# Query norms as softmax scale columns, and queries and keys of a head in turn, in a hybrid attention and mixture-of-experts block

## What is computed

```python
q = rms_norm(q.reshape(B, S, DSA_HEADS, DSA_HEAD_DIM), q_norm_g)
k = rms_norm(k.reshape(B, S, DSA_HEADS, DSA_HEAD_DIM), k_norm_g)
...
logits = jnp.einsum('bqhd,bqkhd->bqhk', qb, k_sel) * (DSA_HEAD_DIM ** -0.5)
logits = jnp.where(valid[:, :, None, :], logits, -jnp.inf)
p = jax.nn.softmax(logits, axis=-1)
```

## Time and profile before

| what | value |
|---|---|
| median of 3 runs | 1149.65 us (1147.72 to 1150.21) |
| profiled execution | 1148.97 us, its span 1147.2 us |
| PE busy | 1094.4 us, 95% |
| DVE busy | 562.6 us, 49% |
| ACT busy | 333.0 us, 29% |
| POOL busy | 263.6 us, 23% |
| moved by DMA | 263.77 MB |

### The profile page before, as it was taken

The page is one execution under the profiler, slowest core; times in us unless marked ns, Lnnn a source line. Parts: engine busy times, 40 slices in busy tenths (PEclk is TensorE's granted clock), DMA queues, the critical chain, the costliest instruction groups (busy, mean ns, idle before and its releaser), DMA issues.

```text
span 1147.2 us, 14250 instructions
## 1 busy us (share of the span) xinstructions
PE 1094.4 (95%) x5694; PEld 709.1 (62%) x5694; DVE 562.6 (49%) x1040; ACT 333.0 (29%) x595; POOL 263.6 (23%) x168
## 2 busy tenths in 40 slices
PE   7999999999999999999999958999999999999997
PEld 5779899767689887878877733333333333333332
DVE  4332693498880243348994452333344433333334
ACT  6344723333332455551224301111111111111111
POOL 7423244333223444453334010000000000000000
PEclk9999999999999999999999969999999999999999
DMA  7222233322214322235318489999999999999995
GB/s 190 74 56 75 73 83 102 92 56 74 74 38 111 78 71 55 57 107 186 110 37 351 182 342 410 421 420 420 419 421 421 420 420 420 420 422 420 421 421 230
DMA packets 129617, 263.77 MB, mean 230 GB/s; under 512 B 12736, under 2 KB 98752, under 8 KB 104976
## 3 DMA queue, kind: packets, MB, share of 16 engines
q1 hardware_dynamic: 125376, 255.23, 59.7%
q0 software_dynamic: 2496, 4.50, 1.1%
q10 hardware_dynamic: 1680, 3.15, 0.7%
HBM read 262.85 MB, written 4.20 MB: 233 GB/s over the span
## 4 chain that ended last, share of the span: by engine, by line
PE 69%; SPq 17%; DVE 6%; DMA 3%; issue 1%; ACT 1%; POOL 1%; DVEq 0%; POOLq 0%; ACTq 0%
PE bank L502 15%; PE bank L523 14%; PE bank L870 10%; SPq L435 9%; PE bank L750 8%; PE bank L884 5%; SPq L436 5%; PE bank L811 3%; SPq L444 3%; DMA arena<-w_exp_up_in 3%; DVE work L1354 2%; PE bank L890 2%; PE bank L706 1%; PE bank L689 1%; PE bank L891 1%
## 5 line engine op out<-in xcount | busy, mean ns | idle before, releaser
L1768 POOL TENSOR_TENSOR piece_r<-arena,piece_r 128x1024 fp32r<-128x1024 f32 x84 | 202.1, 2413 | 329.0 <-ACT piece_r L973 328.9
L870 PE MATMUL bank<-arena,work 128*64 128x512 f32 x1024 | 230.8, 600 | 11.5 <-DMA arena<-w_exp_up_in 10.4
L502 PE MATMUL bank<-piece_r 128*128 128x512 f32 x936 | 232.2, 399 | 0.0
L502 PEld LDWEIGHTS bank<-piece_r 128*128 128x128 f32 x936 | 171.1, 188 | 40.2 <-issue 6.9
L870 PEld LDWEIGHTS bank<-arena,work 128*64 128x64 f32 x1024 | 70.5, 137 | 156.1 <-issue 133.8
L523 PEld LDWEIGHTS bank<-piece_r 128*128 128x128 f32 x1344 | 162.0, 192 | 6.1 <-issue 6.1
L523 PE MATMUL bank<-piece_r 128*128 128x256 f32 x1344 | 164.9, 284 | 0.0
L1640 DVE TENSOR_TENSOR arena<-bank,arena 128x512 f32<-128x512 f32 x128 | 81.8, 683 | 99.1 <-PE bank L891 99.1
L973 ACT ACTIVATE piece_r<-arena 128x1024 fp32r<-128x1024 f32 x84 | 88.4, 1057 | 124.2 <-DMA arena<-w_in_in 68.7
L884 PE MATMUL bank<-arena,bias 128*64 128x512 f32 x512 | 116.9, 598 | 1.6 <-ACT bias L1209 1.4
L1830 POOL DMA_INDIRECT arena<-x_rows,idx_pair x16 | 16.0, 998 | 393.7 <-PE bank L859 345.3
(11 more groups left out here) (244 smaller groups left out, 1085.0 us busy)
## 6 DMA issues: line engine op xcount, KB each, us to landing
arena<-w_exp_gate_in SPq DMA_DIRECT2D x64, 1024.0 KB, 26.1
arena<-w_exp_up_in SPq DMA_DIRECT2D x64, 1024.0 KB, 26.8
arena<-w_exp_down_in SPq DMA_DIRECT2D x32, 2048.0 KB, 29.0
arena<-w_in_in SPq DMA_DIRECT2D x68, 512.0 KB, 3.9
arena<-w_branch_gla_in SPq DMA_DIRECT2D x8, 512.0 KB, 3.9
arena<-w_branch_dsa_in SPq DMA_DIRECT2D x8, 512.0 KB, 5.1
arena<-w_out_in SPq DMA_DIRECT2D x2, 2048.0 KB, 12.6
arena<-x_in SPq DMA_DIRECT2D x4, 512.0 KB, 5.0
```

Source lines behind the costliest of these rows:

```text
L502: last = mm(bank[n % 2][:, :], w[:, k, :], h[:, k, :], start=(i == 0 and k == 0), stop=(i == 2 and k == K - 1))
L870: last = mm(bank[0][hf * WIDE:(hf + 1) * WIDE, :], hTe[q][:, k, :], wgu[sl][2][:, :, k, hf * HALF:(hf + 1) * HALF], start=(k == 0), stop=( ...
L1768: Q.tensor_tensor(quarter(w_lo, q), quarter(w_raw, q), quarter(w_hi, q).bitcast(F32), ALU.subtract).then_inc(s["wlo_ready"], 1)
```

## The change

Queries and keys of a head now come in turn: tile j belongs to head j // 2, and is a query tile for even j and a key tile for odd j. Weight loads, the g column and the place in `qk` follow this order.

A key tile is treated as before. For a query tile the norm is no longer multiplied into the features. The mean squares are made with the frames on the partitions: four matmuls, each with 128 frames of the squares as stationary matrix and one column of the constant matrix as moving one, into four columns of PSUM. ACT takes the root of 128 x 4, DVE its reciprocal and a factor, and the result `q_scale` has one column for each unit. In the softmax the exponential takes that column as its scale in place of a number, and the bias column becomes the negative maximum times that column, an operation with two tensor inputs in SBUF.

```diff
-                mm(bank[2][:, :], mean_m[:, :], sq[j % 2], start=True, stop=True).then_inc(s["qk_ms_ready"], 1)
+                if head_of(j)[1]:
+                    last = mm(bank[2][:, :], mean_m[:, :], sq[j % 2], start=True, stop=True)
+                else:
+                    for t in range(T):
+                        last = mm(bank[2][:, t:t + 1], sq[j % 2][:, t * P:(t + 1) * P], mean_m[:, 0:1],
+                                  start=True, stop=True)
+                last.then_inc(s["qk_ms_ready"], 1)
...
-                if j >= 2:
-                    act.wait_ge(s["qk_ready"], j - 1)
-                A(rms[j % 2], bank[2][:, :], ACT.Sqrt, bias=eps[:, 0:1]).then_inc(s["qk_rms_ready"], 1)
+                h, key = head_of(j)
+                if key:
+                    if j >= 3:
+                        act.wait_ge(s["qk_ready"], j - 1)
+                    A(rms[h % 2], bank[2][:, :], ACT.Sqrt, bias=eps[:, 0:1]).then_inc(s["qk_rms_ready"], 1)
+                else:
+                    A(q_rms[:, h * T:(h + 1) * T], bank[2][:, 0:T], ACT.Sqrt, bias=eps[:, 0:1])\
+                        .then_inc(s["qk_rms_ready"], 1)
...
-                      scale=float(HD) ** -0.5, accum_out=psm[:, u:u + 1]).then_inc(s["prob_ready"], 1)
+                      scale=q_scale[:, u:u + 1], accum_out=psm[:, u:u + 1]).then_inc(s["prob_ready"], 1)
...
             def finish_norm(j):
+                h, key = head_of(j)
                 dve.wait_ge(s["qk_rms_ready"], j + 1)
-                st.did(V.reciprocal(rms[j % 2], rms[j % 2]))
-                st.settle()
-                V.tensor_tensor(qk[:, j, :], qk[:, j, :], rms[j % 2], ALU.mult).then_inc(s["qk_ready"], 1)
+                if key:
+                    st.did(V.reciprocal(rms[h % 2], rms[h % 2]))
+                    st.settle()
+                    V.tensor_tensor(qk[:, H + h, :], qk[:, H + h, :], rms[h % 2], ALU.mult).then_inc(s["qk_ready"], 1)
+                else:
+                    of_head = slice(h * T, (h + 1) * T)
+                    st.did(V.reciprocal(q_scale[:, of_head], q_rms[:, of_head]))
+                    st.settle()
+                    V.tensor_scalar(q_scale[:, of_head], q_scale[:, of_head], float(HD) ** -0.5, None, ALU.mult)\
+                        .then_inc(s["qk_ready"], 1)
...
-                    V.tensor_scalar(nmx[:, u:u + 1], mxl[:, u:u + 1], -float(HD) ** -0.5, None, ALU.mult)\
-                        .then_inc(s["lmax_ready"], 1)
+                    V.scalar_tensor_tensor(nmx[:, u:u + 1], mxl[:, u:u + 1], -1.0, q_scale[:, u:u + 1],
+                                           ALU.mult, ALU.mult).then_inc(s["lmax_ready"], 1)
```

More of the change, by code:

```diff
@@ L256, in encoder_block @@
         psm = sb("psm", [P, T * H])
+        q_rms = sb("q_rms", [P, H * T])
+        q_scale = sb("q_scale", [P, H * T])
         prc = sb("prc", [P, T * H])
@@ L355, in encoder_block, with head_of, qk_place @@
         UNITS = H * T
+        def head_of(j):
+            return j // 2, j % 2 == 1
+        def qk_place(j):
+            h, key = head_of(j)
+            return H + h if key else h
         SMALL_DMAS = 9
@@ L409, in _ @@
                     sp.wait_ge(s["acc_ready"], freed_by(q - 4))
-                    load_quarter(q, wind[:, :, off + q % 4 * P:off + (q % 4 + 1) * P])
+                    at = off + q % 4 * P
+                    if N_Q <= q < N_DV:
+                        h, key = head_of(q - N_Q)
+                        at = (O_DK if key else O_DQ) + h * P
+                    load_quarter(q, wind[:, :, at:at + P])
             for f in range(2):
@@ L1384, in _ @@
                 dve.wait_ge(s["qk_sq_ready"], j + 1)
-                V.tensor_scalar(qk[:, j, :], bank[n % 2][:, :], gqk[:, j // H:j // H + 1], None, ALU.mult)\
+                key = int(head_of(j)[1])
+                V.tensor_scalar(qk[:, qk_place(j), :], bank[n % 2][:, :], gqk[:, key:key + 1], None, ALU.mult)\
                     .then_inc(acc_free[n % 2], 1)
```

## The result

The changed kernel takes 1154.38 us in the median of 20 runs (1151.69 to 1157.57), against 1150.2 us (1147.72 to 1153.96) for 20 runs of the kernel before. The ratio is 1.0037, 95% interval 1.0028 to 1.0045. That is some 4.2 us slower, and outside the range on record.

The account below looks back on a forecast made before the run. PE bounds the kernel up to the experts, then transfers: -1.1 (`pair_out`) - 0.2 (`pair_kv`) + 0.2 (mean squares) + 1.8 (bias column) = +0.7 us on a middle of 1149.3, forecast 1150.0 us, range 1145.5 to 1153.2.

Parts of the forecast that it names:

- These 4.9 us are all that the query and key stage can gain.: Query and key stage: PE's waits for DVE's state update, 3.8 us in `pair_kv` and 1.1 us in `pair_out`, cap the gain.
- The wait of `pair_out` goes: Query and key stage, first round: a query's finish lets `next_states(t, 1)` come early, removing PE's 1.1 us wait.
- So the collision takes back what the freed DVE gives.: Three `pair_kv` waits: the key's multiplication is held behind GpSimd's weight split, so only 0.2 us is gained, not 3.8.
- the second rival: Query and key stage: DVE gets ahead of GpSimd, all three `pair_kv` waits go, 1146.4 us or 1144.6; chance 0.16.
- That is 8 x 0.02 = 0.2 us more, on PE's path.: Query mean squares on PE: each of eight products takes 0.88 us in place of 0.86.
- the one on the same products (loads that don't overlap): Query mean squares on PE: weight loads don't overlap, +5.1 us there, 1154.9 us in all; chance 0.04.
- The bias column's hold: Attention stage: the two-input bias operation is held behind GpSimd's splits, 11 of 32 times, costing 1.8 us at two places.
- the rival without a hold: Attention stage: the one-element bias column isn't held by GpSimd, giving 1148.2 us; chance 0.22.
- Roots and exponentials: ACT: the shorter root is worth nothing; the exponential's second column operand adds 0.09 us each, 2.9 us in all, under cover.
- DVE's busy time falls by some 30 to 40 us: Profile after, whole kernel: DVE would be busy 30 to 40 us less with the time unchanged.
- sign of being wrong: Either PE's attention-stage waits growing by more than 3 us, or the query and key stage shortening by more than 3 us.

Follow-up runs that it names:

- Old order with new norms: The changed kernel with all eight query tiles first, then all eight key tiles, norms as in the changed kernel: 1150.34 us, ratio 0.9994.
- keys first: The changed kernel with the turn reversed, a key tile for even j and a query tile for odd j: 1150.86 us, ratio 0.9999.
- both edits: The changed kernel with the turn reversed (key before query) and the bias column's scale as per-partition operand: 1149.11 us, ratio 0.9987.
- both profiles: Two profiled executions of the changed kernel, the second a repeat with nothing changed: 1154.04 us and 1158.1 us.
- per-partition operand: The changed kernel with the bias column as a tensor_scalar, the scale column not a second tensor input: median 1154.49 us, ratio 1.0027.
- dense work in the wait: The changed kernel with one unused 512-column product before `pair_kv(t, 1)` in rounds t = 1 to 3: 1151.56 us, ratio 1.0001.
- the kernel with the longer wait: The kernel before with an unused 128 x 128 DVE reciprocal ahead of `next_states(t, 0)` for t = 1 to 3: one run of 1156.97 us.

## Why the prediction was wrong, step by step

- *"These 4.9 us are all that the query and key stage can gain."* Borne out. Old order with new norms, keys first and both edits gain 3.5 to 3.8 us there; beyond the waits the stage changes by less than 1 us, for all the 26.8 us of reciprocals taken out.
- *The wait of `pair_out` goes* (-1.1): right, in both profiles.
- *"So the collision takes back what the freed DVE gives."* Right in mechanism and size where GpSimd was ahead, with multiplications of 2.77 to 2.89 us in the five rounds of the two profiles where this was so. It was a race, as the second rival had it, and in one of the two profiles one round went the other way.
- *"That is 8 x 0.02 = 0.2 us more, on PE's path."* This is the step that failed. The step priced the eight products by their length, and the length is right: 0.88 us from the first to `pair_kv` in the kernel with the old order (246.02 to 246.90), the figure of line 609 in the earlier trace rows. It put at nothing what they do to the clock: ahead of a `pair_kv` wait of 1.2 to 1.3 us the granted clock fell to 1.2 GHz in seven of eight cases (two of two and three of three in the changed kernel, two of three with the per-partition operand), at 1.6 us each. In the kernel before the same waits stood behind a dense product and the clock held. Together the step was 0.2 us and should have been 3.4 (two falls) to 5.0 (three). That the two belong together is shown from both sides: dense work in the wait, and the products without a wait, left no fall. That together they are sufficient is not: with keys first they stood ahead of a 1.25 us wait and nothing fell. No rival covered it; the one on the same products (loads that don't overlap) has the right sign and the wrong mechanism, since each block kept its length.
- *The bias column's hold* (+1.8): right, in mechanism, places and size. The kernel before with that one edit measured 1.0016, 1.8 us, and the stage grew by 1.6. The Trainium skill's rule on two SBUF inputs ("SBUF — State Buffer", "Who interferes with whom") is borne out for a single column; the rival without a hold is refuted by durations up to 2349 ns.
- *Roots and exponentials*: the second column operand costs 0.09 us, as said (0.82 us in place of 0.72 for the exponential of 512 columns), and at most 0.2 us of it can be seen in the attention stage.
- *DVE's busy time falls by some 30 to 40 us*: it fell by 26.5, from 562.6 to 536.1. Neither sign of being wrong came: PE's waits for the scaling in the attention stage grew by 1.7 us, and the query and key stage did not shorten. Both signs look at waits and at a gain; the loss in the query and key stage came as TensorE's own work taking longer.

Of the median's 4.2 us, about 1.8 are the bias column. The other 2.4 us are in part argued. In the query and key stage the two profiles give +0.3 (two waits, two falls) and +3.2 us (three and three), but how the 20 runs divide between these cases wasn't seen. Only their mean clock of 0.9856 was, which is 0.0029 below that of before. A fall (3.4 us at half clock in 1150) is 0.0015, so that is about two falls more in a run, wherever they stand. That the lower clock goes with the longer time the 20 runs show themselves: the six at 0.984 took 1155.6 us in the mean, the three at 0.988 1152.4.

Not all of the loss need be in the front. The first profile's span is 5.0 us longer than before, though its first expert load is only 2.2 us late. Another 1.7 us are one more fall at the end, where TensorE has waited for weights: sixteen matmuls there take 5.35 us, against 3.65 in the kernel before. First the changed kernel, then the one before:

```profile
1115.10 5.35 PE bank L891 x16
```
```profile
1111.85 3.65 PE bank L870 x16
```

Such a fall near the end is in five of the seven profiles with the new norms (both of the changed kernel, per-partition operand, dense work in the wait, keys first), and in none of the other two or of the four with the old norms. Whether the change brings it, and why, was not tested; nor was what takes the last 1.1 us.

## What to carry to other kernels

Before making an operation on TensorE thin, look at what stands next to it. Here a thin block of 0.95 us beside a wait of 1.3 mostly brought a fall of 1.6 us, which is more than the wait itself. So less waiting in total can take longer: the changed kernel waited 2.5 us in place of 4.9, and its stage was no shorter. Unused dense work in the wait is a test for this; here 0.86 us of it fitted into waits of 1.3 and cost the stage nothing.

And count tensor inputs: a small DVE operation with a second tensor in SBUF waits for GpSimd as a large one does, while the same number as a per-partition operand did not make it wait. That holds for the bias column and is no pass for every operation with one tensor input: the scaling (line 1430) has one tensor input and a per-partition operand too, and its 384 columns took 1.98 us behind GpSimd at 393.05, against 0.42 for the same form after GpSimd's end in the changed kernel.

## What the runs showed of the hardware that I had not expected

- TensorE's clock fell although the engine was counted busy for 9.06 of the 10.4 us before. Products with one moving column are busy time in the profile, yet in the changed kernel 0.95 us of them and 1.34 of waiting went ahead of a fall as 2.2 us of pure waiting did in the kernel with the longer wait. A single wait of 1.3 us behind a dense product never did, in the kernel before and in the two of its variants that keep it (nine waits).
- The condition is not sharp from outside. Three rounds with the same pattern gave three falls in one execution, and two in the kernel with the per-partition operand and in that with the longer wait; with keys first 2.19 us of it gave none.
- Which of DVE and GpSimd gets into SBUF first is decided by 0.1 us or less. The 512-column multiplication won with a recorded lead of 0.01 and 0.07 us, and lost when 0.06 us behind. The recorded starts don't settle it for every operation: in the kernel before, the 128-column scaling at 400.97 was recorded 0.03 us ahead of GpSimd (401.00, 1.29 us) and still took 1.41 us. The loser pays about what the winner has left: DVE 2.9 us in place of 0.7, or GpSimd 2.9 in place of 2.4.
